# Condition pieces in eight places of their own, loads and panel splits of a transformer kernel in another order

## Chip, cores, metric

The kernel runs on one core of one Trainium2 chip. The metric is the time of one execution on the device, in microseconds; lower is better.

## What is computed

Two transformer blocks over one sequence of 512 positions and width 1024, all in float32, each written here in its main steps:

```python
# first block
h = rms_norm(x, g_mix_pre)
q_f, k_f, v_f, f_logit, q_c, k_c, v_c = split(h @ w_in)
o_f = fox_attention(q_f, k_f, v_f, log_sigmoid(f_logit + b_fgate))      # 8 heads
o_c = chunked_rel_attention(q_c, k_c, v_c, rel_bias)                    # 8 heads
x = x + rms_norm(concat(rms_norm(o_f), rms_norm(o_c)) @ w_out, g_mix_post)
x = x + rms_norm(memory_cross_attention(rms_norm(x), rms_norm(mem), w_q, w_kv, w_o))
x = x + rms_norm((silu(g) * u) @ w_down)          # g, u = split(rms_norm(x) @ w_gate_up)
# second block, two layers
ada = silu(c) @ ada_w[l] + ada_b[l]               # shifts, scales, gates of layer l
y = mlstm_mixer(modulate(rmsnorm(x), sh1, sc1))   # layer 0; layer 1: mla_mixer
x = x + g1 * rmsnorm(y)
x = x + g2 * rmsnorm(square(relu(h2 @ w1)) @ w2)  # h2 = modulate(rmsnorm(x), sh2, sc2)
```

`silu(c) @ ada_w` (with the shared keys' `kv_ada_w`) is a product of a vector with a matrix of 1024 by 14336. The host lays it out as 112 **pieces** of 128 x 1024.

## The kernel before

**Layout.** Activations lie transposed: channels on the 128 partitions, the 512 positions along the free axis, in 8 chunks (`KC`). Each weight is cut into **panels** of 128 x 1024 (512 KB). The matrix products keep float32 precision from parts of a lower one: a panel is copied by ScalarE into its high part `WH` (`panel_high`, L1378), GpSimd writes what is left into `WL` (`split_low`, L658), and TensorE takes three products of parts (`three`, L776 to L778). One chunk of output is 8 x 3 matmuls of 128x512 into one PSUM bank. The eight banks are `G` (0 and 1), `T` (2, 3), `O` (4, 5), `ST` (6) and `AD` (7).

**Stages**, in order on TensorE: `w_in` (16 chunks of queries and keys, then gate logits and values), attention `self` (64 steps, `s`), memory keys, `w_out`, memory values, `mem_q`, attention `mem`, `mem_o`, the gated feed-forward `ffn` (11 groups of 6 panels), `a_in`, `a_og`, values, the mLSTM cells, `a_out`, the feed-forward `mlp0` (16 groups of 4 panels), the latent projections, attention `mla`, `b_out`, `mlp1` (like `mlp0`).

**What sets the order.** Each engine's program is written out by hand, and semaphores join them; every queue runs in program order. SP issues all transfers. `load_panel(p)` waits until panel p-2 is split (`s_split`), since `stage` has two places. `load_piece(q)` waits until piece q-2 was used (`s_pused`), since `apiece` has two. VectorE multiplies a piece by `cond` and sums it into one column of `adac` (`piece`, L2071). ScalarE's `used(p)` waits until TensorE is through panel p and then makes the high part of panel p+2.

**Projections in `JOINT`** (`project`): chunks 0 and 1 run together in banks G[0] and G[1] (`pair_of`), as the input chunks of `H` arrive; the panels of chunks 2 and 3 have places of their own (`WX` or `WZ`, made by `extra_high` and `split_extra`). Chunk c then waits (`bank_free`) until chunk c-2 was taken out of its bank: high part by ScalarE (`evacuate_high`, L1451), low part by VectorE (`evacuate_low`, L2167). An input chunk is made in turns: VectorE scales (L2012), ScalarE writes the high part (L1430), VectorE the low one (L2006).

**Feed-forward.** Group g: `up(g)` in two halves j, `hidden` (ScalarE, VectorE, ScalarE, VectorE write `HID`, L2232 to L2238), `down(g)`, whose eight results VectorE adds to `Y` (L2248). TensorE's order is up(g+1), down(g). Ungated, the halves lie in G[0] and G[1], and half j of up(g) waits for hidden(g-1, j).

**Attention `self`.** Each eight steps handle two heads. At step s TensorE turns the probabilities of step s (`turn`, L950), makes the scores of step s+4, and in the first four of eight steps weighs the values of the two heads before (`weigh`, pieces 0 to 3 a head, 512 to 128 columns wide). `exp` and `pt_high` (L1549) are ScalarE's, `scale` (L690) GpSimd's, `out` takes the result of a head.

`warm` (L868) are matmuls whose result nobody reads.

## Time and profile before

| | |
|---|---|
| median of 3 runs | 2257.38 us (2252.97 to 2259.53) |
| the profiled execution | 2257.02 us |
| its span, first to last instruction | 2255.2 us |
| mean granted TensorE clock | 0.973 of 2.4 GHz |
| TensorE busy | 2127.5 us, 94% of the span |
| VectorE, ScalarE, GpSimd busy | 48%, 39%, 42% |
| moved by DMA | 234.38 MB, 104 GB/s over the span |
| chain that ended last | 72% of it on TensorE |

A row of a timeline gives the start and the length in us, the engine, the line of the kernel, the operation, what it writes and reads, and in brackets how long the engine sat idle before it and what released it. The time that TensorE doesn't work, and the time that it works at half clock, are what can be won; an idle time of another engine costs nothing by itself.

### The profile page before, as it was taken

The page shows a single profiled execution, that of the slowest core. Times are in us where ns is not written, and L with a number is a line of the kernel's source. Part 1 is how long each engine was busy: PE and PEld are TensorE (multiplying, and loading weights), DVE is VectorE, ACT ScalarE, POOL GpSimd, SP SyncE. Part 2 cuts the span into 40 slices and gives each one's busy share as a digit, 9 for nine tenths or more (in the row PEclk, how much of TensorE's full clock was granted, in tenths as well). Part 3 has the DMA queues.
Part 4 walks back from the last instruction along what each step waited for, and adds up shares of the span by engine and source line. Part 5 has one row for each costly group of instructions (what it writes and reads, how often), then busy time and mean ns, then how long its engine had stood idle before and what let it go on. Part 6 is the DMA issues. An engine that isn't in the chain of part 4 may idle for free.

```text
span 2255.2 us, 27272 instructions
## 1 busy us (share of the span) xinstructions
PE 2127.5 (94%) x9534; PEld 1693.5 (75%) x9534; DVE 1087.3 (48%) x1672; ACT 876.0 (39%) x1442; POOL 958.2 (42%) x489
## 2 busy tenths in 40 slices
PE   5899889889999999889998999999999999999997
PEld 3777678677788888667766688888777776888886
DVE  2753661422465556655364543343565425343435
ACT  4224774344422222424265423222465544232332
POOL 2335676353344444423313344444435533444443
PEclk8999999999999999999999999999998999999999
DMA  4671034112254454347102223323222012233322
GB/s 172 211 266 45 20 116 146 57 37 75 66 179 159 156 171 164 112 159 262 65 1 69 67 84 95 101 93 95 91 78 72 1 47 66 88 98 93 100 95 84
DMA packets 66607, 234.38 MB, mean 104 GB/s; under 512 B 7136, under 2 KB 8416, under 8 KB 66400
## 3 DMA queue, kind: packets, MB, share of 16 engines
q1 hardware_dynamic: 66528, 233.33, 31.7%
q8 instruction: 49, 0.80, 0.1%
q14 instruction: 30, 0.25, 0.0%
HBM read 231.20 MB, written 2.10 MB: 103 GB/s over the span
## 4 chain that ended last, share of the span: by engine, by line
PE 72%; issue 13%; DVE 5%; ACT 5%; POOL 4%; DMA 1%; POOLq 0%; SPq 0%; DVEq 0%; ACTq 0%
PE bank L776 22%; PE bank L777 21%; PE bank L778 21%; POOL WL L658 3%; PE bank L883 2%; PE bank L868 1%; PE bank L950 1%; DVE H L2006 1%; DVE bank L2012 1%; PE bank L1017 1%; DVE Y L2248 0%; ACT Y L1556 0%; PE bank L889 0%; PE bank L1051 0%; PE bank L1276 0%
## 5 line engine op out<-in xcount | busy, mean ns | idle before, releaser
L658 POOL TENSOR_TENSOR WL<-stage,WH 128x1024 fp32r<-128x1024 f32 x272 | 660.6, 2429 | 1028.2 <-ACT WH L1378 1028.1
L1378 ACT ACTIVATE WH<-stage 128x1024 fp32r<-128x1024 f32 x272 | 288.2, 1060 | 918.6 <-PE bank L778 881.0
L776 PE MATMUL bank<-H,WH 128*128 128x512 f32 x1324 | 522.0, 394 | 25.3 <-DVE H L2006 11.8
L777 PE MATMUL bank<-H,WH 128*128 128x512 f32 x1324 | 519.4, 392 | 0.0
L778 PE MATMUL bank<-H,WL 128*128 128x512 f32 x1324 | 518.9, 392 | 0.0
L776 PEld LDWEIGHTS bank<-H,WH 128*128 128x128 f32 x1324 | 250.8, 189 | 84.9 <-issue 30.6
L778 PEld LDWEIGHTS bank<-H,WL 128*128 128x128 f32 x1324 | 250.8, 189 | 52.6
L777 PEld LDWEIGHTS bank<-H,WH 128*128 128x128 f32 x1324 | 250.9, 190 | 52.1 <-issue 0.5
L776 PE MATMUL bank<-HID,WH 128*128 128x512 f32 x688 | 268.8, 391 | 5.4 <-DVE Y L2248 5.4
L2248 DVE TENSOR_TENSOR Y<-bank,Y 128x512 f32<-128x512 f32 x344 | 226.3, 685 | 97.3 <-PE bank L778 96.4
L778 PE MATMUL bank<-HID,WL 128*128 128x512 f32 x688 | 268.4, 390 | 0.0
L777 PE MATMUL bank<-HID,WH 128*128 128x512 f32 x688 | 268.4, 390 | 0.0
L2071 DVE SCALAR_TENSOR_TENSOR apiece<-apiece,cond 128x1024 f32<-128x1024 f32 x112 | 184.9, 1665 | 106.9 <-DMA apiece<-ada 106.7
L2234 DVE SCALAR_TENSOR_TENSOR t<-bank,t 128x512 f32<-128x512 f32 x64 | 44.3, 692 | 276.5 <-ACT t L1599 276.4
L776 PEld LDWEIGHTS bank<-HID,WH 128*128 128x128 f32 x688 | 129.6, 188 | 32.5 <-issue 5.8
L2238 DVE TENSOR_TENSOR HID<-t,HID 128x512 fp32r<-128x512 f32 x86 | 121.3, 1411 | 65.0 <-ACT HID L1604 65.0
L777 PEld LDWEIGHTS bank<-HID,WH 128*128 128x128 f32 x688 | 129.7, 188 | 26.9
L778 PEld LDWEIGHTS bank<-HID,WL 128*128 128x128 f32 x688 | 129.5, 188 | 26.9
L868 PE MATMUL bank<-onesr,identr 128*128 128x512 f32 x284 | 81.8, 426 | 0.0
L690 POOL TENSOR_SCALAR sq<-sq,stat 128x256 f32<-128x256 f32 (+2 forms) x56 | 71.5, 1286 | 19.2 <-DVE stat L2183 19.1
L2177 DVE TENSOR_REDUCE stat<-bank 128x1 f32<-128x128 f32 (+3 forms) x112 | 53.3, 477 | 49.4 <-PE bank L1023 22.6
L1604 ACT ACTIVATE HID<-t 128x512 fp32r<-128x512 f32 x86 | 54.2, 631 | 56.3 <-DVE t L2234 50.6
(394 smaller groups left out, 3075.8 us busy)
## 6 DMA issues: line engine op xcount, KB each, us to landing
stage<-panels SPq DMA_DIRECT2D x296, 512.0 KB, 3.5
apiece<-ada SPq DMA_DIRECT2D x112, 512.0 KB, 4.3
RAW<-panels SPq DMA_DIRECT2D x18, 512.0 KB, 3.8
x<-xT SPq DMA_DIRECT2D x4, 1024.0 KB, 7.8
outT<-x SPq DMA_DIRECT2D x8, 256.0 KB, 2.0
Y<-bias SPq DMA_DIRECT2D x1, 1024.0 KB, 4.8
V<-memT SPq DMA_DIRECT2D x2, 512.0 KB, 4.5
con<-cons SPq DMA_DIRECT2D x1, 517.0 KB, 6.7
```

The source lines that it names most:

```text
L658: pool.tensor_tensor(low_of(p, slot), stage[:, slot, :], high_of(p, slot).bitcast(F32), ALU.subtract).then_inc(s_split, 1)
L690: pool.tensor_scalar(prob[b][:, 0:w], prob[b][:, 0:w], stat[:, 8 + b:9 + b], None, ALU.mult)\
L776: pe.matmul(out, wh, rh, start=start, stop=False)
L777: pe.matmul(out, wh, rl, start=False, stop=False)
L778: return pe.matmul(out, wl, rh, start=False, stop=stop)
L868: pe.matmul(out[:, :], identr[:, :], onesr[:, :].rearrange("p (a b) -> p a b", a=1).to_broadcast([P, 4, P]), start=True, stop=True)
L1378: act.activation(high_of(p, slot), stage[:, slot, :], ACT.Copy).then_inc(s_hisplit, 1)
L1604: act.activation(HID[:, slot, j, 0, :], t[:, j, :], ACT.Copy).then_inc(sm["high"], 1)
L2071: dve.scalar_tensor_tensor(apiece[:, k % 2, :], apiece[:, k % 2, :], 1.0, cond[:], ALU.mult, ALU.mult, accum_out=adac[:, column]).then_inc ...
L2177: dve.tensor_reduce(stat[:, b:b + 1], score_bank[b][:, 0:w], AX, ALU.max, negate=True)\
L2238: dve.tensor_tensor(HID[:, slot, j, 1, :], t[:, j, :], HID[:, slot, j, 0, :].bitcast(F32), ALU.subtract).then_inc(sm["split"], 1)
L2248: dve.tensor_tensor(Y[:, m, :], (T + O)[m % 4][:, :], Y[:, m, :], ALU.add)\
```

## The change

- **Start.** `x` comes in three transfers instead of two, the constants in two: the first 256 columns (identity and ones, `s_ones`) after the first part of `x`, the rest after the vectors and the first two panels. TensorE's first sums wait for `s_ones` only. ScalarE makes the high parts of panels 2 and 3 between the input chunks (after m = 4 and m = 6) instead of around them, and the silu of the condition after chunk 0 was taken out.
- **Own banks.** In the projections of `JOINT`, chunks 2 and 3 go to `ST` and `AD` (`own_bank`) and wait for no bank. The ungated feed-forwards change between G[0], G[1] and `ST`, `AD` from group to group, and wait for the hidden values of group g-2.
- **Pieces.** 16 pieces are taken during `w_in` (two after each second chunk from 4 on, and four after the gates), 72 in `ffn`, 24 in `a_in`; before, 40, 40 and 32. From piece 16 on they lie in `ahead`, eight places. In `ffn` VectorE takes four between the two halves of `hidden` and four after the adds, and none after the adds of the tenth group; before, four after the adds of each of ten groups. The queue of SP is ordered anew in the three stages.
- **Attention `self`.** The weighing is spread over steps 0, 1, 3, 4, 5 and 6 of eight (`WEIGHED_AT`); `out` and the next `stage_v` come at steps 6 and 7 instead of 4 and 5, and three norm steps one later.
- **Memory.** The high parts of the first two panels of `mem_q` are made within the squares of `x_mem`, those of the next two within its input chunks.
- **`mla`.** 12 `warm` matmuls ahead of the attention's waits.

```diff
+AHEAD0 = 16
+AHEAD1 = 88
+X_PARTS = [range(0, 2), range(2, 4), range(4, 8)]
...
+WEIGHED_AT = [[(0, 0), (0, 1)], [(1, 0), (1, 1)], [], [(0, 2)], [(1, 2)], [(0, 3)], [(1, 3)], []]
...
+        ahead = place(88, "ahead", [P, 8, D])
...
+        def own_bank(name, c):
+
+            return [ST, AD][c - 2] if name in JOINT and c in (2, 3) else G[c % 2]
...
-                return 8 * (n // 2) + (1, 2, 5, 6)[piece] + 2 * (n % 2)
+                return 8 * (n // 2) + ((1, 2, 5, 7), (3, 4, 6, 8))[n % 2][piece]
...
         def _(sp):
-            sp.dma_start(x[:, 0:4, :], xT[0:4 * P, :].rearrange("(c p) t -> p c t", p=P)).then_inc(s_x, 16)
-            sp.dma_start(con[:], cons).then_inc(s_const, 16)
-            sp.dma_start(x[:, 4:8, :], xT[4 * P:8 * P, :].rearrange("(c p) t -> p c t", p=P)).then_inc(s_x2, 16)
+            for at, part in enumerate(X_PARTS):
+                sp.dma_start(x[:, part.start:part.stop, :],
+                             xT[part.start * P:part.stop * P, :].rearrange("(c p) t -> p c t", p=P))\
+                    .then_inc(s_x[at], 16)
+                if at == 0:
+                    sp.dma_start(con[:, 0:CON["mask"]], cons[:, 0:CON["mask"]]).then_inc(s_ones, 16)
             sp.dma_start(vec[:], vecs).then_inc(s_const, 16)
+            for slot in range(2):
+                sp.dma_start(stage[:, slot, :], panels[slot]).then_inc(s_stage[slot], 16)
+            sp.dma_start(con[:, CON["mask"]:NCON], cons[:, CON["mask"]:NCON]).then_inc(s_const, 16)
+            sp.dma_start(cond[:], c).then_inc(s_c, 16)
+            sp.dma_start(wgate[:], gates_w).then_inc(s_gw, 16)
 
...
-            sp.dma_start(cond[:], c).then_inc(s_c, 16)
-            sp.dma_start(wgate[:], gates_w).then_inc(s_gw, 16)
-            start_pieces(0, 0)
+            plain(2, 6)
             sp.wait_ge(s_h, row(MAKES, "x")[1])
             sp.dma_start(Y[:, 0:4, :].rearrange("p a b -> p (a b)"), bias).then_inc(s_bias, 16)
-            with_pieces(4, 2, 4)
-            end_pieces(20, 34, 6)
+            load_piece(0)
+            load_piece(1)
+            plain(6, 8)
+            for pair in range(1, 8):
+                load_piece(2 * pair)
+                load_piece(2 * pair + 1)
+                plain(2 * pair + 6, 2 * pair + 8)
+            plain(22, 26)
...
-            p0, q0 = PANEL0["ffn"], 40
-            plain(p0, p0 + 12)
-            load_piece(q0, 0)
-            load_piece(q0 + 1, 1)
-            with sp.Fori(0, 4) as i:
-                for half in range(2):
-                    for j in range(6):
-                        load_panel(i * 12 + (p0 + 12 + 6 * half + j), j % 2)
-                        if j < 4:
-                            load_piece(i * 8 + (q0 + 2 + 4 * half + j), j % 2)
...
+            p0 = PANEL0["ffn"]
+            plain(p0, p0 + 4)
+            for k in range(4):
+                load_ahead(AHEAD0 + k, k)
+            plain(p0 + 4, p0 + 6)
+            for k in range(4, 8):
+                load_ahead(AHEAD0 + k, k)
+            plain(p0 + 6, p0 + 10)
+            with sp.Fori(0, 8) as i:
+                for j in range(6):
+                    load_panel(i * 6 + (p0 + 10 + j), j % 2)
+                    for k in ((), (0, 1), (2, 3), (), (4, 5), (6, 7))[j]:
+                        load_ahead(i * 8 + (AHEAD0 + 8 + k), k)
+            plain(p0 + 58, p0 + 68)
+            p0 = PANEL0["a_in"]
+            plain(p0 + 2, p0 + 6)
+            for pair in range(12):
+                for q in (AHEAD1 + 2 * pair, AHEAD1 + 2 * pair + 1):
+                    load_ahead(q, (q - AHEAD0) % 8)
+                load_panel(p0 + 6 + pair, pair % 2)
+            plain(p0 + 18, p0 + 24)
...
-                        if s >= 12 and s % 8 == 5 and s // 8 + 1 < 8:
+                        if s >= 12 and s % 8 == 7 and s // 8 + 1 < 8:
...
-                bank_free(pe, name, c)
+                if isinstance(c, int) and c in (2, 3) and name in JOINT:
+                    held = own_bank(name, c)
+                else:
+                    bank_free(pe, name, c)
+                    held = G[slot]
                 for k in range(KC):
                     input_chunk(fresh, k)
-                    last = three(G[slot][:, 0:width], wh[:, k * P:(k + 1) * P], wl[:, k * P:(k + 1) * P],
+                    last = three(held[:, 0:width], wh[:, k * P:(k + 1) * P], wl[:, k * P:(k + 1) * P],
...
-                        if s >= 8 and s % 8 < 4:
-                            n, piece = 2 * (s // 8 - 1) + s % 2, s % 8 // 2 * 2
-                            weigh(n, piece)
-                            weigh(n, piece + 1)
+                        if s >= 8:
+                            for h, piece in WEIGHED_AT[s % 8]:
+                                weigh(2 * (s // 8 - 1) + h, piece)
                         continue
...
-                banks = [G[0], G[1], ST, AD] if gated else [G[0], None, G[1], None]
...
+                    banks = [G[0], G[1], ST, AD] if gated else [(G[0], ST)[slot], None, (G[1], AD)[slot], None]
...
-                            if not (isinstance(g, int) and g == 0):
+                            if gated and not (isinstance(g, int) and g == 0):
                                 pe.wait_ge(sm["hidden"], g * 2 + j - 1)
+                            if not gated and not (isinstance(g, int) and g < 2):
+                                pe.wait_ge(sm["hidden"], g * 2 + j - 3)
...
-            pe.wait_ge(s_const, 32)
+            pe.wait_ge(s_ones, 16)
...
             pe.wait_ge(s_vev, before(VTILES, "kv_b") + 2 * NT + 1)
+            warm(AD, 12)
             pe.wait_ge(s_qd, 9)
...
-                        if s >= 12 and s % 8 in (4, 5):
+                        if s >= 12 and s % 8 in (6, 7):
...
-            squares("x", xc, lambda m: act.wait_ge(s_x if m < 4 else s_x2, 16))
+            squares("x", xc, lambda m: [act.wait_ge(s_x[at], 16) for at, part in enumerate(X_PARTS) if part.start == m])
             panel_high(0, 0)
             panel_high(1, 1)
             root("x")
+            act.wait_ge(s_ones, 16)
             act.wait_ge(s_const, 32)
-            extra_high("w_in", 0)
-            high("x", scaled_in, hh, lambda m: col("zero"))
-            extra_high("w_in", 1)
+            for m in range(KC):
+                high_chunk("x", m, scaled_in, hh, lambda m: col("zero"))
+                if m in (4, 6):
+                    extra_high("w_in", (m - 4) // 2)
...
-            act.wait_ge(s_c, 16)
-            act.activation(cond[:], cond[:], ACT.Silu).then_inc(s_cond, 1)
-            load_ln_exp()
...
+                if c == 0:
+                    act.wait_ge(s_c, 16)
+                    act.activation(cond[:], cond[:], ACT.Silu).then_inc(s_cond, 1)
+                    load_ln_exp()
...
+                if m in (3, 5):
+                    act.wait_ge(s_used, PANEL0["mem_v"] + (m - 3) // 2 + 1)
+                    panel_high(RING1 + (m - 3) // 2, (m - 3) // 2)
...
-            panel_high(RING1, 0)
-            panel_high(RING1 + 1, 1)
...
             for m in range(KC):
                 high_chunk("x_mem", m, scaled_mem_in, hh, lambda m: col("zero"))
+                if m in (2, 5):
+                    act.wait_ge(s_used, RING1 - 1 + (m - 2) // 3)
+                    extra_high("mem_q", (m - 2) // 3)
             memory_values(1)
-            extra_high("mem_q", 0)
-            extra_high("mem_q", 1)
...
+                def two_groups(i, last=False):
+                    hidden(i * 2 + 1, 1, lambda: pieces(i, 0, range(0, 4)))
+                    add(i * 2)
+                    pieces(i, 0, range(4, 8))
+                    hidden(i * 2 + 2, 0, None if last else lambda: pieces(i, 1, range(0, 4)))
+                    add(i * 2 + 1)
+                    if not last:
+                        pieces(i, 1, range(4, 8))
...
-                for q in (2 * c, 2 * c + 1):
-                    piece(q, 16 * (q // 2 + 1), slice(q, q + 1))
+                if c == 0:
+                    dve.wait_ge(s_cond, 1)
+                if c >= 4 and c % 2 == 0:
+                    piece(c - 4)
+                    piece(c - 3)
                 if c == 3:
...
-            adaptive(4, 1)
+            for q in range(12, AHEAD0):
+                piece(q)
+            add_bias(0, 2)
...
-                for q in (80 + 2 * c, 81 + 2 * c):
-                    piece(q, 16 * (q // 2 + 1), slice(q, q + 1))
-            adaptive(12, 2)
-            add_bias(10, 2)
+                if c >= 4:
+                    piece_ahead(AHEAD1 + 2 * (c - 4))
+                    piece_ahead(AHEAD1 + 2 * (c - 4) + 1)
+            for q in range(AHEAD1 + 8, 112):
+                piece_ahead(q)
+            add_bias(11, 3)
```


On SP's queue, the start of the program before:

```order
L533 DMA x<-xT 128x4x512
L534 DMA con<-cons 128x1034
L535 DMA x<-xT 128x4x512
L536 DMA vec<-vecs 128x293
L581 DMA cond<-c 128x1024
L582 DMA wgate<-gates_w 128x192
L541 DMA stage<-panels 128x1024
L546 DMA apiece<-ada 128x1024
L541 DMA stage<-panels 128x1024
L546 DMA apiece<-ada 128x1024
L541 DMA stage<-panels 128x1024 x2
```

and now:

```order
L545 DMA x<-xT 128x2x512
L549 DMA con<-cons 128x256
L545 DMA x<-xT 128x2x512
L545 DMA x<-xT 128x4x512
L550 DMA vec<-vecs 128x293
L552 DMA stage<-panels 128x1024 x2
L553 DMA con<-cons 128x778
L554 DMA cond<-c 128x1024
L555 DMA wgate<-gates_w 128x192
```

The first transfer of `x` is half as long, the ones come second, and the first panels stand ahead of the condition and with no pieces among them.

On ScalarE, from behind the squares of `x` to the first input chunks before (`WX` are panels 2 and 3, `H` the input chunks):

```order
L1406 ACTIVATE sq<-x 128x512 x8
L1378 ACTIVATE WH<-stage 128x1024 x2
L1421 ACTIVATE logs<-bank,eps 128x512
L1424 ACTIVATE bank<-logs 128x512
L1378 ACTIVATE WX<-stage 128x1024
L1430 ACTIVATE H<-bank,vec 128x512 x8
L1378 ACTIVATE WX<-stage 128x1024
```

and now:

```order
L1388 ACTIVATE WH<-stage 128x1024 x2
L1431 ACTIVATE logs<-bank,eps 128x512
L1434 ACTIVATE bank<-logs 128x512
L1440 ACTIVATE H<-bank,vec 128x512 x5
L1388 ACTIVATE WX<-stage 128x1024
L1440 ACTIVATE H<-bank,vec 128x512 x2
L1388 ACTIVATE WX<-stage 128x1024
L1440 ACTIVATE H<-bank,vec 128x512
L1684 ACTIVATE identr<-con 128x128
L1685 ACTIVATE onesr<-con 128x128
L1686 ACTIVATE maskr<-con 128x128
L1688 ACTIVATE wgateH<-wgate 128x192
```

The high part of panel 2 stood ahead of the first input chunk and stands behind the fifth.

On TensorE, the end of the pair of chunks 0 and 1 and the start of chunk 2 of `w_in` before:

```order
L776 MATMUL bank1<-H,WH 128x512
L777 MATMUL bank1<-H,WH 128x512
L778 MATMUL bank1<-H,WL 128x512
L776 MATMUL bank0<-H,WX 128x512
L777 MATMUL bank0<-H,WX 128x512
L778 MATMUL bank0<-H,WX 128x512
```

and now:

```order
L781 MATMUL bank1<-H,WH 128x512
L782 MATMUL bank1<-H,WH 128x512
L783 MATMUL bank1<-H,WL 128x512
L781 MATMUL bank6<-H,WX 128x512
L782 MATMUL bank6<-H,WX 128x512
L783 MATMUL bank6<-H,WX 128x512
```

Chunk 2 moved from bank 0, which chunk 0 holds, to bank 6.

On VectorE, the end of the tenth group of `ffn` before (`apiece` is a piece, the last `Y` are the adds of the last group):

```order
L2071 SCALAR_TENSOR_TENSOR apiece,adac<-apiece,cond 128x1024
L2071 ISA
L2071 SCALAR_TENSOR_TENSOR apiece,adac<-apiece,cond 128x1024
L2070 REGISTER_ALU
L2071 ISA
L2071 SCALAR_TENSOR_TENSOR apiece,adac<-apiece,cond 128x1024
L2071 ISA
L2071 SCALAR_TENSOR_TENSOR apiece,adac<-apiece,cond 128x1024
L2254 REGISTER_ALU
L2254 COMPARE_AND_BRANCH
L2248 TENSOR_TENSOR Y<-bank,Y 128x512 x3
L1982 TENSOR_TENSOR bank<-sq 128x512
```

and the last two groups now:

```order
L2252 TENSOR_TENSOR t<-bank,t 128x512
L2258 TENSOR_TENSOR HID<-t,HID 128x512
L2086 SCALAR_TENSOR_TENSOR ahead,adac<-ahead,cond 128x1024 x4
L2252 TENSOR_TENSOR t<-bank,t 128x512
L2258 TENSOR_TENSOR HID<-t,HID 128x512
L2268 TENSOR_TENSOR Y<-bank,Y 128x512 x8
L2086 SCALAR_TENSOR_TENSOR ahead,adac<-ahead,cond 128x1024 x4
L2252 TENSOR_TENSOR t<-bank,t 128x512
L2258 TENSOR_TENSOR HID<-t,HID 128x512
L2252 TENSOR_TENSOR t<-bank,t 128x512
L2258 TENSOR_TENSOR HID<-t,HID 128x512
L2268 TENSOR_TENSOR Y<-bank,Y 128x512 x11
```

Four pieces stand between the halves of a group's `hidden` (`t`, `HID`), four behind eight adds, and none ahead of the last adds.

## Rows read from the trace of the kernel before

**Rows 1.** The page: span, granted clock and GB/s in 40 slices, panel loads.
```profile
span 2255.2 us, 27272 instructions
...
PEclk8999999999999999999999999999998999999999
...
GB/s 172 211 266 45 20 116 146 57 37 75 66 179 159 156 171 164 112 159 262 65 1 69 67 84 95 101 93 95 91 78 72 1 47 66 88 98 93 100 95 84
...
stage<-panels SPq DMA_DIRECT2D x296, 512.0 KB, 3.5
```

**Rows 2.** Timeline, start of the program, on ScalarE, GpSimd, VectorE and TensorE.
```profile
6.73 1.15 ACT L1406 ACTIVATE sq<-x 128x512 f32<-128x512 f32 x2 [4.73 <-DMA x<-xT]
...
22.18 0.67 ACT L1421 ACTIVATE logs<-bank,eps 128x512 f32<-128x512 f32 x1
...
27.29 1.06 ACT L1378 ACTIVATE WX<-stage 128x1024 fp32r<-128x1024 f32 x1 [3.81 <-DMA stage<-panels]
...
21.41 4.65 POOL L658 TENSOR_TENSOR WL<-stage,WH 128x1024 fp32r<-128x1024 f32 x2 [20.98 <-ACT WH L1378]
...
23.59 1.41 DVE L2012 SCALAR_TENSOR_TENSOR bank<-x,vec,bank 128x512 f32<-128x512 f32 x2 [22.70 <-ACT bank L1424]
...
11.06 10.50 PE L883 MATMUL bank<-sq,con 128*128 128x512 f32 x16 [11.06 <-DMA vec<-vecs]
...
29.86 0.76 PE L776 MATMUL bank<-H,WH 128*128 128x512 f32 x1 [8.29 <-DVE H L2006]
```

**Rows 3.** TensorE's waits in 30:165, 420:440 and 960:1025; total, times, longest.
```profile
PE bank L776 <- DVE QKL L2167: 11.8, 4, 4.7
...
PE bank L776 <- DVE QKL L2167: 7.3, 1, 7.3
...
PE bank L776 <- DVE QKL L2167: 8.3, 4, 4.0
```

**Rows 4.** Stretches: busy us (instructions) of PE, PEld, DVE, ACT, POOL; clock, DMA share, GB/s.
```profile
59.00:64.80 5.80, 5.74 (x14) 4.52 (x15) 3.97 (x5) 0.00 (x0) 1.13 (x1) 0.50 0.36 120
...
432.30:437.10 4.80, 4.80 (x12) 3.80 (x13) 0.69 (x1) 1.47 (x2) 3.35 (x2) 0.52 0.45 122
...
1283.00:1287.00 4.00, 4.00 (x12) 3.17 (x11) 2.36 (x3) 2.24 (x4) 2.38 (x1) 0.57 0.42 133
```

**Rows 5.** Attention `self`: a stretch of eight steps, and two rows of its timeline.
```profile
237.51:250.66 13.15, 11.46 (x84) 9.15 (x84) 7.82 (x24) 9.30 (x28) 9.83 (x10) 1.00 0.25 81
...
237.51 0.66 PE L950 MATMUL bank<-con,sq 128*128 128x128 f32 x4 [0.96 <-POOL sq L690]
...
239.10 0.60 ACT L1549 ACTIVATE PT<-bank 128x512 fp32r<-128x512 f32 x1
```

**Rows 6.** `ffn`: timeline of VectorE in one group; a stretch; TensorE at the last group.
```profile
640.06 2.47 DVE L2238 TENSOR_TENSOR HID<-t,HID 128x512 fp32r<-128x512 f32 x1 [0.92 <-ACT HID L1604]
...
649.33 0.69 DVE L2232 TENSOR_TENSOR t<-bank,t 128x512 f32<-128x512 f32 x1 [6.79 <-PE bank L778]
...
660.82 1.22 DVE L2071 SCALAR_TENSOR_TENSOR apiece<-apiece,cond 128x1024 f32<-128x1024 f32 x1
...
661.96 3.41 DVE L2071 SCALAR_TENSOR_TENSOR apiece<-apiece,cond 128x1024 f32<-128x1024 f32 x1
...
640.00:672.00 32.00, 32.00 (x142) 26.51 (x142) 18.35 (x20) 7.65 (x10) 14.54 (x6) 1.00 0.47 156
...
932.15 0.76 PE L776 MATMUL bank<-HID,WH 128*128 128x512 f32 x1 [5.42 <-DVE Y L2248]
```

**Rows 7.** Timeline, TensorE at the second group of `mlp0`.
```profile
1282.66 0.47 PE L776 MATMUL bank<-H,WX 128*128 128x512 f32 x1 [2.80 <-DVE t L2234]
```

**Rows 8.** Timeline and stretches, TensorE at the start of attention `mla`.
```profile
1732.93 0.30 PE L776 MATMUL bank<-QKH 128*128 128x128 f32 x1 [2.39 <-DVE ROT L2523]
...
1734.00:1736.00 2.00, 2.00 (x8) 1.55 (x9) 0.29 (x1) 0.98 (x3) 0.69 (x1) 0.50 0.00 0
...
1752.00:1754.00 2.00, 2.00 (x8) 1.54 (x7) 0.56 (x1) 0.95 (x3) 0.00 (x0) 0.50 0.00 0
```

121 lines of the change are left out of this document (47 added, 74 removed).

## Prediction

> **What bounds the kernel.** I read the page first: TensorE is busy 94% of a span of 2255.2 us (the table above), and the granted clock is below 0.9 of full in one of the 40 slices [rows 1]. So the time is TensorE's, and only two things can be won: its idle time (2255.2 - 2127.5 = 128 us) and the stretches that it works at half clock. I then took TensorE's waits one after another, and beside each the clock behind it. The waits that the change aims at stand in five places: the start [rows 2], the projections' third and fourth chunks [rows 3], the end of `ffn` [rows 6], the second group of the two ungated feed-forwards [rows 7], and the start of `mla` [rows 8]. A wait costs more than its length: behind one of some 2 us or more the clock is mostly at half (1.2 of 2.4 GHz) for about four microseconds. In a stretch at clock k, full of matmuls, (1-k) of its length is lost: 5.8 x 0.50 = 2.9 us, 4.8 x 0.48 = 2.3 us, 4.0 x 0.43 = 1.7 us [rows 4].
>
> The sum is made against the profiled execution's own 2257.0 us (1.8 us more than its span); the median of the runs is 0.4 us above it. A measurement of this kernel can't tell a change within 0.3%, 6.8 us, from none.
>
> **Start: -9.0 us.** TensorE's sums wait until 11.06 for the vectors, though the first squares begin at 6.73, and take 10.5 us [rows 2]. Now they need 0.5 MB of `x` and the ones, 0.6 MB where 1.5 MB were in flight, so they begin near 5.7 and end near 16.2. The two panel highs stand ahead of the root, as before, which so comes 5.4 us earlier than at 22.18. Before, the root was followed by scaled chunks from 23.59, but the first matmul of `w_in` came at 29.86, 6.3 us later, since ScalarE first waited 3.81 us for panel 2 and split it [rows 2]. With that split moved behind the fifth chunk, the way takes 2.2 us (two scalings, a high and a low part), so from 18.2 the first matmul could go at 20.4. GpSimd's two splits (4.65 us [rows 2]), begun about a microsecond behind the start of the first panel high, end near 20.8: that is now the last to arrive. 29.9 - 20.8 = 9.0. The two highs inside the chunks delay two of them by 1 us, behind which TensorE, at half clock at first, is late anyway. If the loads come later than I think, 5 us remain; I see no more than 10.
>
> **`w_in`: -17.0.** Four waits of 11.8 us for the low part of a chunk [rows 3], and three half-clock stretches (one is 2.9 us, the others as the last of rows 4, 1.7 each): 18.1. Own banks remove the first two; the others came from VectorE, where two pieces stood behind each chunk, and now two behind each second one. What is late next: SP. It loads panels 8 and on only behind a pair of pieces, whose places come free when VectorE has used the pair before; I get 1.8 us of slack each time, so I take 1 us off. If that slack isn't there, one such wait of 1 to 2 us for each of six pairs returns, 9 us; so 9 to 18.
>
> **Attention `self`: -4.** Eight steps take 13.15 us, in which TensorE is busy 11.46 and no other engine over 9.83 [rows 5]: the order costs 1.7 us. TensorE waits 0.96 us for GpSimd's 512-wide scales, and ScalarE makes the high part of step 6 only at 239.10, though its turn was through at 238.2, because `out` and the staging stand between [rows 5]. The change takes work off TensorE ahead of the scores that these scales wait for (two weighings of 0.3 us) and moves `out` behind. That is up to 1.5 us in each of seven such stretches, 10 in all; but ScalarE's `out` now stands close ahead of the weighing that needs its bank. Nothing in the trace prices that, so the bounds are -9 and +4, and I take -4, nearer to the idle time seen.
>
> **`mem_q`: -8.6.** One wait of 7.3 us [rows 3] and 2.3 us of clock [rows 4]. The two splits within the input chunks hold these up by 1 us in all (each is 1.06 [rows 2], and ScalarE has some idle time in every chunk to catch up). Those moved into the squares lie in ScalarE's waits for VectorE.
>
> **End of `ffn`: -6.1.** TensorE waits 5.42 us [rows 6] and loses 1.7 on the clock, since the last adds stand behind four pieces; now no piece stands there: -7.1. Against it stands what 32 more pieces do inside the groups, beside TensorE's 144 matmuls a group, 32.5 us at 32.00 / 142 = 0.225 us each [rows 6]. A piece takes 1.15 us, but 3.41 where GpSimd splits a panel [rows 6]. Between the halves of `hidden` VectorE is free from 642.5 (640.06 + 2.47) to 649.33, 6.8 us [rows 6]; four pieces with one split across them take 4 x 1.15 + 2.26 = 6.9. It just fits. The four behind the adds stood there before, and no longer wait for their landing. I take 1 us for what sticks out. The Trainium skill (SBUF — State Buffer, "SBUF: two separate sides") says that VectorE's operations with two SBUF inputs and GpSimd's hold a shared port in turn for a whole instruction; the 3.41 agrees, and the rule speaks against more pieces: by it GpSimd's splits too wait for pieces. What that would give is the third rival.
>
> **`a_in`: -11.0.** Four waits of 8.3 us [rows 3], two stretches of 1.7: 11.7, less 0.7 for chunks that may still wait. Its pieces start four chunks later and are loaded ahead in eight places.
>
> **`mlp0`, `mlp1`: -9.0.** Each waits 2.8 us in its second group (the row of `mlp0` in [rows 7]; `mlp1` reads alike) and then loses 1.7 [rows 4]. Up(1) now writes other banks, and down(0) needs the hidden values only two chunks of 24 matmuls later, 10.8 us: nothing is late next.
>
> **`mla`: -8.** Here TensorE waits 2.39 us, and the clock is at half from 1734 to past 1754 [rows 8], with TensorE busy throughout: 20 us whose work takes 10 at full clock. 12 warm matmuls of 0.225 us fill 2.7 us, 0.3 more than the wait: +0.3. I take 8 of 10, for the softmax chain may then limit; the bounds are +0.3 (the clock falls all the same) and -10.
>
> **Sum:** 9.0 + 17.0 + 4.0 + 8.6 + 6.1 + 11.0 + 9.0 + 8.0 = 72.7. 2257.0 - 72.7 = **2184 us**.
>
> **Rivals.**
> 1. *Half the clock's gain doesn't come* (chance 0.18). `mla` stays at half clock (+8) and `self` gives nothing (+4): 2196. For it: the scores there are short matmuls, and once the clock had fallen it took 20 us to return, where elsewhere it took four. Against it: no other place keeps half clock with so little idle time.
> 2. *The SP queue is the next bound in `w_in`* (0.10). Panels behind pieces: +8; with 1 us at each of four places in `a_in`: 2184 + 8 + 4 = 2196, beside the first rival up to 2208.
> 3. *VectorE overloaded in `ffn`* (0.07). If two splits fall into the middle four pieces, `hidden` is 2.3 us late; ScalarE waits for it, and so the next panel's high part. Over nine sets of eight pieces: +20, 2204. By the skill's rule above this is the result if GpSimd's split comes to stand between pieces each time. Against it: a split comes once a chunk, 24 x 0.225 = 5.4 us, and the four take 6.9, so a second one falls in only if they start late.
> 4. *Slower* (0.03): pieces land too late in `ffn`. A group now loads 6 panels and 8 pieces, 14 transfers of 512 KB. VectorE waits in the middle of `hidden`, ScalarE behind it, the panel's high part behind ScalarE, TensorE last. This decides when a set holds TensorE up by 72.7 / 9 = 8.1 us, that is, when a transfer takes over (32.5 + 8.1) / 14 = 2.9 us of the queue; at 3.5 us, the time in which a lone panel lands [rows 1], without overlap, a set takes 49 us: 9 x 16.5 = +148, 2332. Against it: the third slice moved 266 GB/s [rows 1], 2.0 us a transfer.
> 5. *The change doesn't do what it says* (0.02): chunks 2 and 3 wait for their panels' low parts instead of their banks. All of rows 3 returns, 27 us and 12 of clock: 2223.
>
> **How the numbers follow.** The forecast has 0.60, its own spread from the unknown terms being 2174 (all at their good end: `self` 5 more, `mla` 2, the rest 3) to 2193. The range to 2210 takes in rivals 1 to 3, and leaves out about 0.1 above and 0.1 below. Faster by over 0.3% means below 2250.6: everything but rival 4 and a little for the unknown, 0.95; within 0.3%: 0.02; slower: 0.03.
>
> **What the profile would show.** The first matmul of `w_in` near 21 us; in TensorE's waits hardly a row for `QKL` in the three stretches; the wait ahead of `ffn`'s last group gone, and group spacing in `ffn` still 32.5 us (if it is 34 or more, rival 3 or 4); no wait at the second group of `mlp0`; clock 1.00 at the start of `mla` (0.50: rival 1); eight steps of `self` in 12.5 us. I am wrong in kind if the saved waits return behind the pieces' landing, and in size if clock stretches stay where waits went.

## The result, and the profile after

The changed kernel takes 2171.18 us (median of four runs, 2168.62 to 2180.89); the kernel before, run beside it, 2257.03. The ratio is 0.9629 [0.9596, 0.9662]: 85.9 us, 3.8%. The forecast was 2184 us with a range of 2174 to 2210: the direction was right, and the time fell 2.8 us below the range.

The profiled execution took 2168.6 us, 88.4 less than that of before. It is the fastest of the four, so the table below, which is made from it, shows 2.5 us more gain than the medians do. Three lines of its page answer to [rows 1]: the span, TensorE's busy time, and the granted clock in 40 slices, none of which is below 0.9 now.

```profile
span 2166.8 us, 27220 instructions
PE 2091.8 (97%) x9546; PEld 1669.9 (77%) x9546; DVE 1108.0 (51%) x1670; ACT 875.5 (40%) x1442; POOL 973.6 (45%) x489
PEclk9999999999999999999999999999999999999999
```

To find where the time went I took the same instruction of TensorE in both timelines at each stage's edge, and compared the distances:

| from ... to | before | after | gain | forecast |
|---|---|---|---|---|
| start ... first matmul of `w_in` | 29.86 | 19.02 | 10.8 | 9.0 |
| ... first 64x256 scores of `self` | 165.37 | 150.19 | 15.2 | 17.0 |
| ... second head sum behind `self` | 129.93 | 115.37 | 14.6 | 4.0 |
| ... warm matmuls ahead of `mem_q` (`mem_k`, `w_out`, `mem_v`) | 86.96 | 89.01 | -2.1 | 0 |
| ... first score of `mem` (`mem_q`) | 57.61 | 47.47 | 10.1 | 8.6 |
| ... first matmul of `ffn` | 103.11 | 104.31 | -1.2 | 0 |
| ... first sum of `x_a` (`ffn`) | 374.39 | 367.09 | 7.3 | 6.1 |
| ... first guard of the cells (`a_in`) | 186.31 | 173.23 | 13.1 | 11.0 |
| ... first matmul of `mlp0` | 135.17 | 135.96 | -0.8 | 0 |
| ... first sum of `x_b` (`mlp0`) | 360.89 | 356.22 | 4.7 | 4.5 |
| ... first matmul of `b_out` (latents, `mla`) | 192.28 | 180.29 | 12.0 | 8.0 |
| ... end (`mlp1`) | 433.3 | 428.6 | 4.7 | 4.5 |

Two thirds of the miss stand in one line, `self`: 10.6 of 15.7 us. The next is `mla`, with 4.0. The rest of this part shows the rows behind most of the lines that came out otherwise than forecast; `mla` follows among the experiments.

**Start.** Of TensorE (start, duration, instruction, idle time before it and what ended it), and GpSimd's first two low parts, for [rows 2]:

```profile
5.41 9.00 PE L892 MATMUL bank<-sq,con 128*128 128x512 f32 x16 [5.41 <-ACT sq L1416]
19.02 0.77 PE L781 MATMUL bank<-H,WH 128*128 128x512 f32 x1 [4.60 <-POOL WL L663]
14.26 4.65 POOL L663 TENSOR_TENSOR WL<-stage,WH 128x1024 fp32r<-128x1024 f32 x2 [13.83 <-ACT WH L1388]
```

GpSimd is the last to arrive, as forecast, at 18.9 instead of 20.8.

**`self`.** Windows over the whole stretch, and two single slices of before (length, busy time of each engine with its count, granted clock, DMA share, GB/s). The kernel before:

```profile
core 0: us, PE busy (x) PEld busy (x) DVE busy (x) ACT busy (x) POOL busy (x), PEclk, DMA share, GB/s
195.23:325.16 129.93, 109.60 (x731) 87.89 (x731) 80.49 (x224) 90.06 (x250) 92.03 (x77) 0.93 0.11 39
211.23:219.23 8.00, 8.00 (x49) 6.46 (x48) 4.17 (x13) 4.21 (x14) 5.30 (x6) 0.79 0.00 1
307.23:315.23 8.00, 5.26 (x19) 3.74 (x20) 4.50 (x8) 6.00 (x11) 7.27 (x4) 0.71 0.59 237
```

The changed kernel, with the two stretches behind it:

```profile
169.21:284.58 115.37, 103.36 (x732) 82.55 (x732) 77.72 (x224) 90.26 (x250) 92.30 (x77) 1.00 0.12 42
284.58:373.59 89.01, 87.18 (x445) 73.14 (x443) 34.11 (x49) 44.69 (x68) 54.18 (x24) 1.00 0.40 136
373.59:421.06 47.47, 45.11 (x200) 36.91 (x198) 15.25 (x23) 18.80 (x27) 17.96 (x8) 1.00 0.24 78
```

The same matmuls (731 and 732 records) are busy for 109.6 us at a mean clock of 0.93, and for 103.4 at 1.00. So the gain of 14.6 is 8.3 us of idle time (20.3 to 12.0) and 6.2 us of clock. The two single slices are places where before lost some of it. How much of the clock's part would come again is a question for the experiments.

**Ahead of `mem_q`.** VectorE's adds of squares (`acc`) in the changed kernel, GpSimd's low parts of `mem_q`'s first two panels, and TensorE's wait:

```profile
360.15 2.69 POOL L663 TENSOR_TENSOR WL<-stage,WH 128x1024 fp32r<-128x1024 f32 x1
361.29 2.10 DVE L1997 TENSOR_TENSOR acc<-acc,sq 128x512 f32<-128x512 f32 x1
...
365.14 2.48 POOL L663 TENSOR_TENSOR WL<-stage,WH 128x1024 fp32r<-128x1024 f32 x1 [2.30 <-ACT WH L1388]
366.01 2.89 DVE L1997 TENSOR_TENSOR acc<-acc,sq 128x512 f32<-128x512 f32 x2
...
369.04 1.10 PE L898 MATMUL bank<-acc,con 128*128 128x512 f32 x2 [1.83 <-DVE acc L1997]
```

An add takes 0.69 us where GpSimd is idle; here one takes 2.10, and a pair 2.89, each while a GpSimd low part runs. The wait of 1.83 us is the larger part of the loss of 2.1 us in the table; the experiments below show whether the adds make it.

**`a_in`.** Waits by engine and line (us in total, times, longest), in about the first 50 us of the stage, before (960 to 1010) and after (904 to 950). Before:

```profile
ACT WH L1378 <- DMA stage<-panels: 14.2, 2, 9.9
DVE apiece L2071 <- DMA apiece<-ada: 10.9, 6, 2.4
DVE QKL L2167 <- ACT QKH L1451: 10.8, 2, 7.3
```

And on the SP queue of before, what it waited for, and the two entries that it then issued:

```profile
SPq L546 <- DVE apiece L2071: 16.4, 2, 15.8
974.08 1.46 SPq L546 DMA_DIRECT2D apiece<-ada  x2
975.74 0.33 SPq L541 DMA_DIRECT2D stage<-panels  x1
```

After:

```profile
DVE QKL L2184 <- ACT QKH L1461: 21.5, 8, 5.7
ACT WH L1388 <- PE bank L783: 19.2, 5, 4.8
```

Before, the SP queue stood 15.8 us until VectorE had used a piece, then issued two pieces and behind them the panel at 975.74; ScalarE waited 9.9 us for that panel to land, and VectorE 7.3 us for ScalarE. After, ScalarE waits for no panel in the whole stage. The prediction had not looked at ScalarE's waits in this place.

**`w_in`.** Before shows the same chain here. ScalarE's waits for panels, and the SP queue's for a place, in 30 to 165 and in 39 to 60:

```profile
ACT WH L1378 <- DMA stage<-panels: 11.8, 2, 10.5
SPq L546 <- DVE apiece L2071: 10.2, 2, 9.6
```

The changed kernel still waits in `w_in`, though less. ScalarE (high parts), TensorE, and the issues on the SP queue:

```profile
78.73 2.21 SPq L560 DMA_DIRECT2D stage<-panels  x2
...
85.31 1.06 ACT L1388 ACTIVATE WH<-stage 128x1024 fp32r<-128x1024 f32 x1 [6.93 <-DMA stage<-panels]
...
88.96 0.49 PE L781 MATMUL bank<-H,WH 128*128 128x512 f32 x1 [1.27 <-POOL WL L663]
...
98.16 1.06 ACT L1388 ACTIVATE WH<-stage 128x1024 fp32r<-128x1024 f32 x1 [8.90 <-DMA stage<-panels]
...
101.79 0.49 PE L781 MATMUL bank<-H,WH 128*128 128x512 f32 x1 [1.65 <-POOL WL L663]
```

The panel that ScalarE takes at 85.31 was issued at 78.73 or behind, after a pair of pieces that began 1.5 us earlier: some 6 us to its landing, with 2 MB in flight. A third wait of TensorE, 1.41 us at 71.10, names `QKL`. This is the second rival, in part.

### The profile page after: what moved, and what is told of

The parts are those of the page before. It is cut to its first block, busy times and chain, and to the rows that moved or that the text cites. A ratio compares the mean times of both kernels' runs of the same rounds, so it can differ in the third digit from the quotient of the medians.

```text
span 2166.8 us, 27220 instructions
## 1 busy us (share of the span) xinstructions
PE 2091.8 (97%) x9546; PEld 1669.9 (77%) x9546; DVE 1108.0 (51%) x1670; ACT 875.5 (40%) x1442; POOL 973.6 (45%) x489
## 4 chain that ended last, share of the span: by engine, by line
PE 79%; issue 6%; DVE 5%; ACT 4%; POOL 4%; DMA 1%; SPq 0%; POOLq 0%; DVEq 0%; ACTq 0%
PE bank L781 24%; PE bank L783 24%; PE bank L782 24%; PE bank L892 2%; POOL WL L663 2%; PE bank L877 1%; POOL sq L695 1%; PE bank L959 1%; DVE acc L1997 1%; POOL t L695 1%; DVE Y L2268 0%; DVE bank L2070 0%; PE bank L1285 0%; DMA stage<-panels 0%; ACT sq L1416 0%
## 5 line engine op out<-in xcount | busy, mean ns | idle before, releaser
L663 POOL TENSOR_TENSOR WL<-stage,WH 128x1024 fp32r<-128x1024 f32 x272 | 675.5, 2484 | 954.0 <-ACT WH L1388 953.9
L2086 DVE SCALAR_TENSOR_TENSOR ahead<-ahead,cond 128x1024 f32<-128x1024 f32 x96 | 164.9, 1768 | 7.7 <-DMA ahead<-ada 7.7
L2184 DVE SCALAR_TENSOR_TENSOR QKL<-bank,QKH 128x512 fp32r<-128x512 f32 x40 | 27.2, 688 | 101.4 <-ACT QKH L1461 97.9
L695 POOL TENSOR_SCALAR sq<-sq,stat 128x256 f32<-128x256 f32 (+2 forms) x56 | 71.4, 1282 | 16.5 <-DVE stat L2200 16.4
```

The source lines that it names most:

```text
L663: pool.tensor_tensor(low_of(p, slot), stage[:, slot, :], high_of(p, slot).bitcast(F32), ALU.subtract).then_inc(s_split, 1)
L695: pool.tensor_scalar(prob[b][:, 0:w], prob[b][:, 0:w], stat[:, 8 + b:9 + b], None, ALU.mult)\
L2086: dve.scalar_tensor_tensor(source, source, 1.0, cond[:], ALU.mult, ALU.mult, accum_out=adac[:, column])\
```

## Experiments

All are edits of the changed kernel unless they name another. Ratios are to the kernel before, run on the same chip, with a 95% interval; the changed kernel's is 0.9629.

### What makes the gain in `self`

**self_old** puts the order of the attention back:

```diff
-WEIGHED_AT = [[(0, 0), (0, 1)], [(1, 0), (1, 1)], [], [(0, 2)], [(1, 2)], [(0, 3)], [(1, 3)], []]
+WEIGHED_AT = [[(0, 0), (0, 1)], [(1, 0), (1, 1)], [(0, 2), (0, 3)], [(1, 2), (1, 3)], [], [], [], []]
-                        if s >= 12 and s % 8 in (6, 7):
+                        if s >= 12 and s % 8 in (4, 5):
```

and with it `weighed`, `low_v` and the norm steps.

> The changed kernel with the order within attention self put back: both halves of a head weighed close together, out and the staging of values at steps 4 and 5 of eight, the norm steps one earlier. Read on: from the 64x256 scores that open the second set of eight steps to the second head sum behind the attention. That took 129.6 us before and 115.0 us in the changed kernel, 14.6 us less, where the forecast had 4 with bounds of -9 and +4. Theory 1 (the order alone makes the whole of it): 129.6 +- 1, and the program 14 to 15 us longer than the changed kernel, near 2186 us. Theory 2 (a part comes from what goes on ahead of the attention, such as the clock or the loads): under 125 us, and the program less than 10 us longer.

**self_out_later** puts back only the first of these two lines and `weighed`.

> The changed kernel with the old order of weighing alone: both pieces of each half stand one behind the other in the first four of eight steps, while out, the staging and the norm steps stay at the late places of the changed kernel. Theory A (the gain is the late out, which kept ScalarE from the high part of the sixth step): the stretch named above stays within 3 us of 115.0. Theory B (the gain is the spread of the weighing, which stood ahead of the scores for which GpSimd's scales wait): over 126 us, since out was only ever late by its bank. Between: both have a share. My guess is B with two thirds, 124 to 129 us.

Measured: 2186.87 us, ratio 0.9683 [0.9658, 0.9708], and 2177.16 us, 0.9643 [0.9612, 0.9673]. The whole stretch in self_old, and two slices of it:

```profile
170.53:302.98 132.45, 112.38 (x731) 89.73 (x731) 80.64 (x224) 90.49 (x250) 92.25 (x77) 0.91 0.11 38
186.53:194.53 8.00, 7.00 (x33) 5.55 (x34) 3.90 (x13) 3.39 (x13) 5.39 (x6) 0.60 0.00 0
242.53:250.53 8.00, 5.78 (x31) 4.21 (x30) 5.54 (x14) 7.59 (x21) 5.76 (x6) 0.73 0.00 1
```

And in self_out_later:

```profile
168.43:290.91 122.48, 108.31 (x732) 86.42 (x731) 78.57 (x224) 89.93 (x250) 92.53 (x77) 0.94 0.11 41
```

self_old: 132.45 us (129.93 before, from the same first scores), above the 129.6 +- 1 that theory 1 expected, yet its idle time is 20.1 us against 20.3 before. The order makes all of the idle time that the change saved; the 2.5 us on top are the clock, 0.91 where before had 0.93, for the same code and the same waits. self_out_later at 122.5 is in the zone between, and my guess on the shares was wrong. Idle time is 14.2 us: moving `out` and the staging alone takes 5.9 us of 8.1, the spread of the weighing 2.2. The other 5.0 us by which this stretch is longer than the changed kernel's are busy time at a lower clock, and the edit need not be their cause.

Thirteen kernels of this document run the changed order of `self` as it is: the changed kernel and all below but self_old_warmed and filled. Their idle time in the stretch is 11.3 to 12.1 us. Their busy time is 103.3 to 103.4 us in four profiles, the changed kernel's among them, and 104.9 to 109.3 in nine, and the stretch takes 115.2 to 121.2 us. The longest, from order_old_banks_old:

```profile
173.41:294.65 121.24, 109.25 (x731) 87.22 (x731) 77.91 (x224) 90.57 (x250) 92.43 (x77) 0.94 0.12 41
```

So the 8.3 us of idle time belong to the order and repeat. Of the clock's part, against this profile of before, anything from 0.3 to 6.2 us may come, by the execution that is profiled.

**self_old_warmed** tests the clock in the old order:

```diff
+                    if name == "self" and s % 8 == 6:
+                        warm(T[b % 2], 4)
                     pe.wait_ge(sm["probs"], s + 1)
```

> The kernel of self_old (old order within attention self), with four warm matmuls ahead of TensorE's wait for GpSimd's 512-wide scales in every eighth step, where it stood idle for 0.8 to 1.6 us. Stretch from the first 64x256 scores of self to the second head sum: 129.9 us in the kernel before, 132.5 in self_old, 115.4 in the changed kernel. In self_old TensorE's idle time there is 8.6 us above the changed kernel's, and its clock was 0.60 to 0.84 in six of sixteen slices, where the changed kernel's was 1.00 in all. Theory (some 6 to 9 us of the 14.6 are the clock, which falls behind these waits): waits remain filled, clock 0.97 or more in all slices, the stretch 124 to 127 us, the program 6 us shorter than self_old. Rival (the clock has nothing to do with these waits): slices near 0.8 remain and the stretch stays above 130 us; with clock 1.00 and the stretch still above 130 us, the time would be in the dependency chain.

Measured: 2182.40 us, 0.9668 [0.9652, 0.9684].

```profile
168.87:299.06 130.19, 117.94 (x763) 93.17 (x763) 79.75 (x224) 90.21 (x250) 92.58 (x77) 0.93 0.11 38
240.87:248.87 8.00, 8.00 (x39) 6.31 (x39) 4.22 (x8) 4.73 (x14) 2.79 (x4) 0.67 0.01 2
```

2.3 us shorter than self_old, not 6 or more: the theory failed. The stretch stays above 130 us with slices down to 0.67, which is what the rival named; but its reason, that the clock has nothing to do with the waits, isn't shown by it. Waits of 2.19 us near the start, 2.04 us (for VectorE) and 1.78 us (for ScalarE) stood outside the fill, and the slice right behind the last is the one at 0.67. How the 6.2 us of clock divide among the waits stays open; that the clock falls near waits of about 1.6 to 2.2 us in some executions and not in others is what these kernels show beside the changed one.

### What makes the gain in `mem_q` and `a_in`

**memq_splits_old** puts the four panel splits back (two behind the squares, two behind the input chunks), **memq_lows_late** keeps them and lets GpSimd wait:

```diff
+            pool.wait_ge(s_add, before(ADDS, "x_mem") + row(ADDS, "x_mem")[1])
             split_lows(RING1, RING1 + 2)
```

> The changed kernel with the four panel splits ahead of mem_q put back: two between the last square and the root, two behind the eight input chunks. Read on two stretches: from the second head sum to the six warm matmuls (87.0 us before, 89.0 in the changed kernel) and from there to the first score of attention mem (57.6 and 47.5 us). Theory (the order of the splits makes both, the loss of 2 us and the gain of 10.1): 87.0 and 57.6 +- 0.7, the program 8 us longer, near 2179 us. Rival (the 2 us are lost by something else, since the kernel reaches this place 41 us earlier than before): the first stretch stays at 89 us.

> The changed kernel, with GpSimd made to wait for the last add of x_mem before it makes the low parts of mem_q's first two panels; their high parts stay within the squares. In the changed kernel the adds on VectorE took 2.10 us and 2.89 us for two, where 0.69 is usual, at the same time as GpSimd's low parts at 360.15 and 365.14, and TensorE then waited 1.83 us for the adds. Theory (GpSimd's work holds VectorE's adds up): all adds 0.7 us, the wait under 0.4 us, the stretch to the warm matmuls 87.2 us, the program 1 to 2 us shorter. Rival (the high parts on ScalarE hold the squares up, GpSimd is innocent): adds still over 1.4 us or the wait still over 1.2 us. Second rival: the wait moves on to the first matmul of mem_q, which then waits some 1 to 2 us for a low part, so that the program stays the same.

Measured: 2171.59 us, 0.9613 [0.9580, 0.9645], and 2169.98 us, 0.9609 [0.9581, 0.9637]. From the sums of `mix` to the warm matmuls ahead of `mem_q` both take 21.70 us, as before, where the changed kernel takes 23.76. So the loss of 2.1 us belongs to the splits' new order, and within it to GpSimd: with its low parts behind the adds

```profile
368.62 4.72 POOL L663 TENSOR_TENSOR WL<-stage,WH 128x1024 fp32r<-128x1024 f32 x2 [6.13 <-DVE acc L1998]
```

the adds take 0.7 us and TensorE doesn't wait, nor does it later (`mem_q` 47.43 us). In the program's time the 2.1 us don't stand out: the intervals of the ratios overlap. The high parts on ScalarE are innocent. The Trainium skill (SBUF — State Buffer, "SBUF: two separate sides") says that a VectorE operation with two SBUF inputs and a GpSimd operation that reads SBUF exclude each other for a whole instruction; the trace agrees, with 2.10 us for an add beside a low part.

But `mem_q` itself took 48.85 us with the old splits, not the 57.6 expected. The order of the splits is not what gave 10 us. **no_own_banks** removes the other candidate:

```diff
-            return [ST, AD][c - 2] if name in JOINT and c in (2, 3) else G[c % 2]
+            return G[c % 2]
```

and TensorE waits (`bank_free`) ahead of chunks 2 and 3 again.

> The changed kernel without the banks of their own for chunks 2 and 3 of w_in, mem_q and a_in: they take G[0] and G[1] again and wait for chunks 0 and 1. Theory (the banks make the gain in mem_q, where the order of the splits gave nothing): from the warm matmuls to the first score of mem 56 to 58 us instead of 47.5, one wait near 7 us for QKL. In w_in and a_in two waits each of 3 to 4 us return, with a half-clock stretch at one or two of them; the other two do not, as VectorE has no pieces there now. Program 20 to 27 us longer, 2191 to 2198 us. Rival (the pieces' move alone would have been enough in w_in and a_in): only mem_q returns, 2181 us.

Measured: 2181.23 us, 0.9664 [0.9638, 0.9689]; `mem_q` 49.6 us, `w_in` 153.2 instead of 150.2, `a_in` 164.3 instead of 161.7. Far less than expected, again. Profiles of the same code differ here too: with own banks `w_in` took 148.8 to 151.8 us in eleven kernels and `a_in` 161.6 to 163.3 in twelve, and without them `w_in` took 152.1 to 153.2 in three. So both edits were undone together, and in `a_in` the pieces put back behind each chunk from the first: **order_old_banks_kept** and **order_old_banks_old**.

```diff
-                if c >= 4:
-                    piece_ahead(AHEAD1 + 2 * (c - 4))
-                    piece_ahead(AHEAD1 + 2 * (c - 4) + 1)
+                piece_ahead(AHEAD1 + 2 * c)
+                piece_ahead(AHEAD1 + 2 * c + 1)
```

On the SP queue the pieces of `a_in` then begin two panels earlier.

> The changed kernel with the old order in two places, its own banks kept: mem_q's four splits as before, and a_in's pieces two behind each chunk from the first on. Read on: from the warm matmuls ahead of mem_q to the first score of mem (57.6 us before, 47.5 changed, 48.9 with the old splits alone) and from the first matmul of a_in to the first guard of the cells (174.7 before, 161.7 changed, 164.3 without own banks). Theory (bank and order are two remedies for one wait, and either is enough): 48.9 and 162 to 165 us. Rival (the pieces' move makes the gain in a_in): 170 us or more there.

> The same old order, now without the own banks. Theory (either remedy alone is enough, so each undone alone showed 2 to 3 us, and both undone show all): mem_q 57 to 58 us with a wait of about 7 us, a_in 173 to 175 us with four waits for QKL, 8 us in all; the program 20 us or more longer than the changed kernel, that is, far more than the sum of the two single edits in mem_q (1.4 + 2.1 us). Rival (a third part of the change makes these gains, such as earlier loads): mem_q stays under 52 us.

Measured: 2173.77 us, 0.9615 [0.9591, 0.9639], and 2189.51 us, 0.9679 [0.9650, 0.9708]. `mem_q`: 48.9 and 57.9 us. With both undone the wait of before [rows 3] is back to the hundredth:

```profile
401.36 0.77 PE L781 MATMUL bank<-H,WZ 128*128 128x512 f32 x1 [7.30 <-DVE QKL L2179]
```

ScalarE, which makes each chunk's high part, first waits for a panel to land. Its waits in `mem_q`, with old splits and own banks (memq_splits_old):

```profile
ACT WH L1388 <- DMA stage<-panels: 6.2, 2, 5.3
```

And with both old (order_old_banks_old):

```profile
ACT WH L1385 <- DMA stage<-panels: 6.1, 2, 5.3
```

The wait of 5.3 us is there in both; with two more banks TensorE works through it, and with the new order of the splits the longest is 0.3 us (changed kernel and no_own_banks). Bank and order are two remedies for one wait. In `a_in` the picture is another: 161.7 and 165.0 us from the first matmul to the first guard, where the kernel before took 174.7 and the second expectation had 173 to 175. Early pieces with own banks cost nothing, and without own banks 3.3 us. Ten microseconds had neither cause.

**a_in_two_places** and **a_in_two_places_old_banks** (with early pieces, and with own banks and without) let the SP queue wait as if there were two places:

```diff
-                    sp.wait_ge(s_pused, q - 7)
+                    sp.wait_ge(s_pused, q - (1 if isinstance(q, int) and q >= AHEAD1 + 2 else 7))
```

> The changed kernel with a_in's pieces two behind each chunk from the first on, and the SP queue made to wait before each of them until the piece but one before it is used, as if there were two places; the own banks are kept. The stretch from a_in's first matmul to the first guard of the cells was 174.7 us before, 161.7 in the changed kernel and with early pieces, 165.0 with early pieces and old banks, so 10 us have another cause. In the kernel before, ScalarE there waited 9.90 us for a panel that stood on the SP queue behind pieces waiting for their place, and evacuated its bank only behind that panel's split. Theory (the eight places free the queue, and that is the gain): ScalarE waits 4 us or more for panels again; with own banks TensorE is spared a part, 164 to 172 us. Rival (places don't matter): 162 us.

> The same without own banks. Theory: the whole of the time before returns, 172 to 176 us, with four waits for QKL of 8 us in all and ScalarE's wait of 8 to 10 us for a panel. Rival (places don't matter): 165 us, as with early pieces and old banks.

Measured: 2197.94 us, 0.9724 [0.9708, 0.9739], and 2198.82 us, 0.9724 [0.9707, 0.9741]; `a_in` 183.6 and 186.0 us. The waits of the first, in the chunks of `a_in`:

```profile
DVE ahead L2086 <- DMA ahead<-ada: 21.2, 5, 5.1
ACT WH L1388 <- DMA stage<-panels: 15.4, 2, 11.2
PE bank L781 <- DVE QKL L2184: 12.1, 4, 7.6
```

The places are a third cause: with two, ScalarE waits 11.2 us for a panel again, as the theory said, and own banks spare only 2.4 us. It went further than either expectation, 9 to 11 us past the kernel before, and ScalarE waits for panels late in the stage too, up to 5.4 us. One difference to that kernel is known: here the two pieces of a pair share a semaphore, so the first waits for the landing of both. I didn't test it. So it is shown that two places make the wait for the panel, and not shown that they make just the ten microseconds of before.

**w_in_panels_first** uses the same insight the other way:

```diff
             for pair in range(1, 8):
+                plain(2 * pair + 6, 2 * pair + 8)
                 load_piece(2 * pair)
                 load_piece(2 * pair + 1)
-                plain(2 * pair + 6, 2 * pair + 8)
```

> The changed kernel, with each pair of panels of w_in issued on the SP queue ahead of its pair of pieces instead of behind. In the changed kernel ScalarE waited 6.7 to 9.7 us for each second panel to land and TensorE 1.27 and 1.65 us for their low parts. Theory (the pair of pieces in front of the panels makes them late): ScalarE's waits for panels shrink by some 3 us, TensorE's two waits go, w_in 2 to 4 us shorter, the program 2168 us. Rival (the pieces come late instead, and VectorE waits for them ahead of the low part of a chunk): waits of TensorE for QKL of 1 us or more, the program the same or 2 to 6 us longer.

Measured: 2170.61 us, 0.9608 [0.9590, 0.9626]. `w_in` takes 145.55 us instead of 150.19, and TensorE's three waits of 1.3 to 1.7 us are gone; in reordered and filled, which have this edit too, it takes 145.8 and 145.1. In the profiled execution 3.0 of these 4.6 us were lost again in `self`, where the clock fell at the start (first eight steps 16.5 us instead of 14.6), and the program's median, 0.6 us less than the changed kernel's, doesn't show the gain.

### What makes the gain in `mla`

**mla_no_warm** takes `warm(AD, 12)` out.

> The changed kernel without the twelve warm matmuls ahead of attention mla. From the first matmul behind the last wait for GpSimd to the first wait of the attention's end the kernel before took 85.8 us and the changed one 76.9. Theory (the wait of 2.4 us lets the clock fall for twenty microseconds of short matmuls): 85 to 87 us, clock 0.5 for some 20 us, the program 9 us longer, near 2180 us. Rival (the clock there depends on what came before, and the changed kernel comes with fewer waits): 77 us, no difference.

Measured: 2181.74 us, 0.9667 [0.9651, 0.9684]; from the first sum of `x_b` to `b_out` 189.1 us instead of 180.3, so 8.8 us. The first score without the warm matmuls, and a window over what follows:

```profile
1662.61 0.30 PE L781 MATMUL bank<-QKH 128*128 128x128 f32 x1 [2.40 <-DVE ROT L2554]
```

```profile
1660.00:1692.00 32.00, 29.60 (x128) 22.21 (x128) 12.12 (x33) 11.98 (x35) 11.76 (x11) 0.79 0.03 11
```

And the twelve matmuls of the changed kernel, with its window:

```profile
1657.07 2.90 PE L877 MATMUL bank<-onesr,identr 128*128 128x512 f32 x12
```

```profile
1657.00:1690.00 33.00, 33.00 (x181) 25.55 (x179) 15.33 (x42) 15.19 (x44) 17.29 (x16) 1.00 0.03 11
```

The twelve matmuls take up the wait of 2.40 us, and the clock stays at 1.00. The first rival is refuted for `mla`.

Not all of the 8.8 us are the fill's. From the first score to the last weighing of values `mla` took 83.2 us before and 80.2 in mla_no_warm, and 74.1 in all sixteen kernels with the fill: 6.1 us, less 0.2 to 0.3 by which the matmuls lengthen the way into it. The other 3 us lie in two places that the edit doesn't touch: the way from `x_b` to the first score, and the one from the last weighing to `b_out`. There the clock differs from profile to profile. With the same code the whole stretch took 180.3 to 180.5 us in eight kernels, the changed one among them, and 183.3 to 183.7 in seven.

### Is VectorE near its limit in `ffn`?

**ffn_held_2** and **ffn_held_6** put a reduction over 2048 or 6144 elements behind the four middle pieces, nine times:

```diff
+                            if k == 3:
+                                dve.tensor_reduce(stat[:, 8:8 + 2], cond[:].rearrange("p (a b) -> p a b", a=1).to_broadcast([P, 2, D]), AX, ALU.max)
```

> The changed kernel with an extra reduction over 2048 elements on VectorE behind the four middle pieces of each of nine sets in ffn, some 2.2 us, which makes the second half of hidden late by that. The third rival of the prediction priced 2.3 us of lateness at 2.3 us for each set: +20 us. Read on: from the first matmul of ffn to the first sum of x_a, 367.1 us in the changed kernel. Theory (hidden values and the next panel's split have slack of some 3 us on ScalarE and more on TensorE, the rival's price was wrong): 367 to 368 us. By the rival's price: 387 us.

> The same with a reduction over 6144 elements, some 6.5 us, nine times. Theory (slack of about 3.9 us on ScalarE up to its next panel, and 1.9 us more until TensorE needs that panel's low part): TensorE waits 0 to 3 us a set, the stretch 370 to 390 us, and its waits name GpSimd's low part or the hidden values. If all lateness counted: 367 + 9 x 6.5 = 426 us. If it stays at 367, the slack is above 6.5 us.

Measured: 2171.46 us, 0.9618 [0.9592, 0.9644], and 2229.30 us, 0.9862 [0.9828, 0.9895]. `ffn` takes 367.1 us with the short hold, and 421.1 with the long one: 54.0 us, 6.0 a set. The long reduction takes 6.54 us. TensorE's wait, nine times alike, and the eight microseconds behind the first:

```profile
582.40 0.61 PE L781 MATMUL bank<-HID,WH 128*128 128x512 f32 x1 [3.77 <-DVE Y L2270]
```

```profile
582.40:590.40 8.00, 8.00 (x28) 6.46 (x29) 4.38 (x8) 0.67 (x1) 1.93 (x1) 0.79 0.56 200
```

Of 6.5 us, 3.77 reach TensorE as a wait, nine times 33.9 us in all, and the other 20 of the 54 us are clock, 2.2 a set (1.7 behind the first: 0.79 over 8 us). So there are about 2.7 us of slack (6.5 - 3.77), and 2.2 us cost nothing. The long hold cost more than the 3 us a set that I had as its upper end. I had put the slack at 3.9 and 1.9 us up to the next panel's low part, but TensorE's wait names VectorE's adds, which come late together with the hidden values, and the clock I hadn't priced at all.

### A version that beats both

**reordered** joins w_in_panels_first and memq_lows_late; **filled** adds warm matmuls in seven waits:

```diff
+            warm(AD, 11)
             project("mem_o", 8, "o_mem")
...
+            warm(AD, 9)
             project("b_out", 8, "o_b")
...
+            warm(AD, 14)
             with pe.Fori(1, 4) as i:
...
-                        warm(O[1], 4)
+                        warm(O[1], 12 if name == "self" and s == 0 else 4)
```

and 7 at step 6 of `self`, 5 ahead of the last weighing of `mem` and `mla`.

> The changed kernel with two edits that each gave something alone: w_in's panels ahead of its pieces on the SP queue (w_in 4.6 us shorter), and GpSimd's low parts of mem_q's first panels behind the adds of x_mem (2.1 us shorter). If the gains stand, 6.5 us less than the changed kernel, 2164 to 2165 us. Rival (a wait of 1.62 to 2.19 us at the start of self lets the clock fall in some runs and not in others: its first eight steps took 14.6 us in four kernels and 15.1 to 17.7 in ten): 2165 to 2170 us.

> The kernel above with warm matmuls in TensorE's waits at the start of self (8 and 7 more), ahead of the last weighing of mem and mla (5), and ahead of mem_o (11), b_out (9) and the third chunk of a_out (14), each sized to the wait that stood there. Theory (the clock falls behind a wait of 2 us or more, and fill keeps it up): no half-clock stretch at these places, where the changed kernel lost 1.1, 1.6, 1.6 and 1.5 us and self up to 3; 5 to 8 us less than the kernel above, 2157 to 2160 us. Rival (warm matmuls in front of work delay it as much as they save): the same as the kernel above.

Measured: 2166.04 us, 0.9577 [0.9562, 0.9593], and 2158.94 us, 0.9553 [0.9540, 0.9566]. filled is 7.1 us faster than reordered and some 12 us faster than the changed kernel, as its theory expected; reordered came out at 5.1 us less than the changed kernel by the medians, within its rival's range (by the ratios it is more, 0.9577 against 0.9629). The five runs of filled lie within 1.9 us, those of reordered within 10.4, and no run of reordered is as short as the longest of filled. In the profiles `mem` took 37.3 instead of 40.3 us, `mem_o` 62.7 instead of 64.3, the stretch with `a_out` 134.4 instead of 135.8, and from `b_out` to TensorE's last matmul 414.7 instead of 416.3, each by a half-clock stretch less. `mem` took 37.3 us once without fill, in memq_lows_late, and 38.6 to 40.3 in the others; `mem_o` never took less than 64.1 without it. So the fill makes certain what otherwise comes at times or never. The start of `self` is at 1.00; one wait that was left open there (1.60 us, for VectorE) still costs:

```profile
236.96:244.96 8.00, 8.00 (x42) 6.88 (x43) 5.85 (x17) 5.45 (x17) 7.43 (x5) 0.61 0.00 0
```

## Why the prediction was right, and where it was wrong

**What bounds the kernel**: right. The gain is TensorE's idle time and its clock. TensorE's idle time went from 127.7 us of the span to 75.0, which is 52.7 of the 88.4 us; its busy time fell by the other 35.7 us, at a mean granted clock of 0.973 before and 0.992 after.

**Start, `mlp0` and `mlp1`, the end of `ffn`**: within 2 us each, and the traces agree with the mechanism, but no run undoes these parts singly. The start took 18.9 to 20.7 us in the kernels that share it, so 19.02 is at its short end. The microsecond set aside for pieces that stick out in `ffn` was not needed. By the prediction's own numbers the four pieces took 6.9 us in a gap of 6.8; the slack of 2.7 us behind them made that harmless, and by it the third rival, 2.3 us late at 2.3 us a set, would have cost nothing.

**`mla`: -8**: right in mechanism. From the first score to the last weighing 9.1 us were gained (83.2 to 74.1), and half clock no longer stands there. The table has 12.0, since the clock also stayed up in the two places ahead of and behind it; that was in no term, and in seven other kernels it didn't happen.

**Attention `self`: -4** is the step that failed. Idle time was put at "up to 1.5 us in each of seven such stretches, 10 in all"; then I took 4, "nearer to the idle time seen". Measured are 8.3 of idle time, and 1.3 in the very eight steps of [rows 5] (13.15 to 11.8 us). So the term was mis-sized: it is 8.3 and not 4. By the experiments the later `out` and staging make 5.9 us of it and the spread weighing 2.2. And I had written down a window there whose clock was 1.00, and took it for the whole stretch; the whole stretch ran at 0.93, and what its clock gave back, 6.2 us in this profile, was in no bound. The low end of the range rested on -9 for this term; with the clock counted it would have been -15, and the range would have held the time. How much of the clock's part stands behind the median of 2171.18 us is open: with the same order it was 6.2 us in four profiles and 0.3 to 4.7 in nine.

**`mem_q`: -8.6, `a_in`: -11, `w_in`: -17**: sizes right within 2.1 us, and in part by luck, since the cause was wrong or not asked for. In `w_in` I put two of the four waits down to pieces behind chunks on VectorE, since they named VectorE's `QKL`, and for `a_in` I named later pieces and eight places without asking which of them removes what. `mem_q` has no pieces, and the prediction gives no cause for its wait of 7.3 us. VectorE waited for ScalarE, and ScalarE for a panel's landing; in `a_in` and `w_in` the panel stood on SP behind pieces that waited for one of two places. Own banks, which the prediction named as what removes these waits in `w_in`, give 2 to 3 us of each when they alone are undone; in `mem_q` they would have been nearly enough alone (48.85 us with the old splits). What makes the rest of the 15.2 us in `w_in` no run tests: the trace of before has the same chain as in `a_in`, and the change takes pieces out, sets them later and moves loads there all at once.

**"Those moved into the squares lie in ScalarE's waits for VectorE"** failed: true of the high parts, but each releases a low part on GpSimd, which holds VectorE's adds up; -2.1 us. The prediction's own rule for moved steps, that each instruction it sets off counts, was not followed here.

**SP queue in `w_in`** (second rival, priced at +8): half right. Three waits came, 4.3 us in all, two of them for the low parts of late panels, and panels first removes 4.6 us.

## What to carry to other kernels

When a wait names an engine, follow what that engine waited for, to the DMA if need be, before pricing the remedy: here `QKL` on VectorE meant a panel behind a blocked queue entry. Where a change holds several remedies, undo them together as well as singly: in `mem_q` each alone showed 1 to 2 us of 10. And read the mean clock of a whole stretch beside its idle time; the clock was 6 of 15 us in `self`, and whether such a gain repeats is read from several profiles of the same code. Filling known waits with matmuls sized to them gave 7 us more and runs that agree within 2 us.

## What the runs showed of the hardware

The same code behind the same waits runs at either clock. The first eight steps of `self`, from the first 64x256 scores to the second, contain waits of 2.19 and 1.62 us in all kernels that don't fill them; they took 14.6 us in four profiled executions and 15.1 to 17.7 in eleven, and self_old has the idle time of before, 20.1 us, and 2.5 us more of clock. The length of the wait alone doesn't tell: in the eighteen profiles the clock fell to half behind 17 of 31 waits of 2.35 to 2.45 us, both of those ahead of `mla` among them (before and mla_no_warm), and behind all nine waits of 3.77 us in ffn_held_6. The prediction's sum had taken falls behind such waits as given; it is a matter of how often. The other surprise was the size of GpSimd's hold on VectorE for plain 512-wide adds: from 0.69 to 2.10 us beside a low part that itself took 2.69 instead of 2.40 (the median of 272).
